# GpSimd multiplies the softmax rows of both attentions of block 2 by their reciprocals, and VectorE evicts every second turned tile of the odd one

## The reference, cut to what matters

```
p = softmax(s)          # exp(s - max) / sum, along the keys
out = p @ v
```

## Time and profile before

| | |
|---|---|
| runs | 1958.44, 1960.0, 1961.77 us, median 1960.0 |
| profiled execution | span 1956.7 us from first to last instruction; the page gives no time of it beside this span |
| TensorE busy | 1913.7 us, 98% of the span |
| VectorE, ScalarE, GpSimd busy | 1273.9, 922.8, 14.1 us |
| chain that ended last | TensorE 92%, VectorE 4%, ScalarE 2% |
| granted TensorE clock | 0.995 on average |
| DMA | 320.62 MB, mean 164 GB/s |

### The profile page before, as it was taken

One profiled execution on the slowest core, in us unless ns is written; L12 is line 12 of the kernel. 1 busy time (PEld: TensorE's weight loads), 2 busy tenths in 40 slices (PEclk: granted clock), 3 DMA queues, 4 the chain that ended last, 5 costly groups with the idle time before them and its releaser, 6 DMA issues.

```text
span 1956.7 us, 28779 instructions
## 1 busy us (share of the span) xinstructions
PE 1913.7 (98%) x11994; PEld 1629.3 (83%) x11994; DVE 1273.9 (65%) x1670; ACT 922.8 (47%) x1300; POOL 14.1 (1%) x17
## 2 busy tenths in 40 slices
PE   7999999999999999999999999999999999989998
PEld 6888969888888888788879878988888889679997
DVE  5776796766676668776664464765554367757774
ACT  5334565334533455643454355543333345755553
POOL 0000000000000000000000110000000000000000
PEclk9999999999999999999999999999999999999999
DMA  7876536765476642776453211222323223024552
GB/s 279 283 274 218 186 105 224 280 257 216 157 277 253 229 174 95 272 274 252 152 174 107 108 44 65 101 94 86 108 86 108 87 86 109 23 86 165 180 194 87
DMA packets 46065, 320.62 MB, mean 164 GB/s; under 512 B 5233, under 2 KB 5361, under 8 KB 7921
## 3 DMA queue, kind: packets, MB, share of 16 engines
q1 hardware_dynamic: 39024, 270.09, 38.4%
q10 hardware_dynamic: 6912, 48.69, 6.5%
HBM read 317.72 MB, written 1.05 MB: 163 GB/s over the span
## 4 chain that ended last, share of the span: by engine, by line
PE 92%; DVE 4%; ACT 2%; issue 1%; DMA 0%; DVEq 0%; ACTq 0%
PE ps L532 89%; PE ps L873 1%; DVE s_big L2181 1%; DVE s_wl L1890 1%; PE ps L734 0%; ACT s_wh L1228 0%; PE ps L711 0%; DVE s_st L2120 0%; ACT s_big L1398 0%; DVE s_tmp L2410 0%; DVE ps L2114 0%; DVE s_X L2386 0%; PE ps L835 0%; DVE s_X L2076 0%; DMA s_X<-in_x 0%
## 5 line engine op out<-in xcount | busy, mean ns | idle before, releaser
L532 PE MATMUL ps<-s_xx,s_wh 128*128 128x512 f32 (+1 forms) x3328 | 899.6, 348 | 11.2 <-DVE s_wl L1960 10.0
L1890 DVE TENSOR_TENSOR s_wl<-s_raw,s_wh 128x2048 fp32r<-128x2048 f32 x213 | 487.4, 2290 | 293.5 <-ACT s_wh L1228 293.4
L532 PE MATMUL ps<-s_xx,s_wl 128*128 128x256 f32 (+1 forms) x2208 | 670.2, 304 | 0.4 <-DVE s_xx L2413 0.4
L532 PEld LDWEIGHTS ps<-s_xx,s_wh 128*128 128x128 f32 x3328 | 579.7, 190 | 106.4 <-DVE s_wl L1960 10.3
L1228 ACT ACTIVATE s_wh<-s_raw 128x2048 fp32r<-128x2048 f32 x213 | 404.7, 1907 | 133.0 <-PE ps L532 129.7
L532 PEld LDWEIGHTS ps<-s_xx,s_wl 128*128 128x128 f32 x2208 | 419.4, 190 | 19.6 <-issue 3.2
L532 PE MATMUL ps<-s_wh,s_hl 128*128 128x512 f32 (+1 forms) x608 | 232.3, 382 | 0.5 <-DVE s_hl L1982 0.5
L532 PE MATMUL ps<-s_wh,s_hh 128*128 128x512 f32 (+1 forms) x608 | 230.0, 378 | 0.0
L532 PE MATMUL ps<-s_wl,s_hh 128*128 128x512 f32 (+1 forms) x608 | 229.8, 378 | 0.0
L532 PE MATMUL ps<-s_wh,s_xx 128*128 128x256 f32 x928 | 179.4, 287 | 0.0
L1342 ACT ACTIVATE s_tmp<-s_tmp 128x512 f32<-128x512 f32 x44 | 27.8, 632 | 281.2 <-DVE s_tmp L2007 274.5
(11 more groups left out here) (235 smaller groups left out, 1680.9 us busy)
## 6 DMA issues: line engine op xcount, KB each, us to landing
s_big<-in_w_ada ACTq DMA_DIRECT2D x46, 1024.0 KB, 6.1
s_raw<-in_ffn_down SPq DMA_DIRECT2D x44, 1024.0 KB, 4.8
s_raw<-in_w_up SPq DMA_DIRECT2D x44, 1024.0 KB, 4.8
s_raw<-in_ffn_gate SPq DMA_DIRECT2D x43, 1024.0 KB, 5.1
s_raw<-in_ffn_up SPq DMA_DIRECT2D x43, 1024.0 KB, 4.8
s_raw<-in_w_down SPq DMA_DIRECT2D x22, 1024.0 KB, 4.8
s_raw<-in_w_in SPq DMA_DIRECT2D x18, 1024.0 KB, 4.8
s_raw<-in_w_in_ab SPq DMA_DIRECT2D x10, 1024.0 KB, 4.8
```

The costliest lines, as they stand in the source:

```text
L532: return pe.matmul(o, lhsT, rhs, start=start, stop=stop, skip_group_check=True)
L1890: dve.tensor_tensor(wide(wl, u), raw[:, u % SLOTS, :].rearrange("p (k n) -> p k n", k=8), f32(wide(wh, u)), SUB).then_inc(*w_low.tick(u))
```

## The change

GpSimd gets a function `weigh(A, u)` that does the multiplications that `unit_divide` did on VectorE, in place and with the same operands, for both attentions; VectorE keeps the reciprocal. A new signal `weighed` is waited for by TensorE before it turns a tile, and by VectorE before it overwrites statistics of eight units earlier. GpSimd's program is ordered by hand: bias additions of heads 0 to 3, `weigh(0)`, heads 4 and 5, `weigh(1)`, `weigh(2)`, heads 6 and 7, `weigh(3)`, and then the rest in order.

In the odd attention (`A.both == 1`) ScalarE evicts only the turned tile of i = 0; VectorE evicts that of i = 1 with a copy, after `unit_maxima(n)` and before `out_low(n-3)`, and raises the new signal `brought`, for which TensorE waits before the values. In the even attention ScalarE keeps both evictions.

```diff
@@ class Attention
-                self.units = []
+                self.units, self.both = [], 2 if name == "even" else 1
@@ tensor, unit_turns
-                    pe.wait_ge(*divided[A.name, u, i])
+                    pe.wait_ge(*weighed[A.name, u, i])
...
-                    freed[b] = turned[A.name, u, i]
+                    freed[b] = (turned if i < A.both else brought)[A.name, u, i]
@@ tensor, unit_values
-                pe.wait_ge(*turned[A.name, u, 1])
+                pe.wait_ge(*turned[A.name, u, A.both - 1])
+                if A.both == 1:
+                    pe.wait_ge(*brought[A.name, u, 1])
@@ scalar, unit_turned
-                for i, hd in A.pair_of(u):
+                for i in range(A.both):
@@ vector, unit_maxima
                     if u >= 8:
-                        dve.wait_ge(*divided[A.name, u - 8, 1])
+                        dve.wait_ge(*weighed[A.name, u - 8, 1])
@@ vector, unit_divide
                 dve.reciprocal(A.stat(u, "over", n=2 * n), A.stat(u, "sum", n=2 * n)).then_inc(
-                    *divided.tick((A.name, u, "r")))
-                dve.wait_ge(*divided[A.name, u, "r"])
-                for i, hd in A.pair_of(u):
-                    for j, (q, off, w) in enumerate(A.parts(u)):
-                        e = A.e(u, i)[:, off:off + w]
-                        dve.tensor_scalar(e, e, A.stat(u, "over", i, j), None, MUL).then_inc(
-                            *divided.tick((A.name, u, i)))
+                    *divided.tick((A.name, u)))
@@ vector, attend
                     unit_maxima(A, n)
+                if A.both == 1 and 2 <= n < len(A.units) + 2:
+                    dve.wait_ge(*product[A.name, "t", n - 2, 1])
+                    if n >= 4:
+                        dve.wait_ge(*product[A.name, "pv", n - 4])
+                    src, dst = A.turn(n - 2, 1)
+                    dve.tensor_copy(dst, src).then_inc(*brought.tick((A.name, n - 2, 1)))
@@ gpsimd
+            def weigh(A, u):
+                pool.wait_ge(*divided[A.name, u])
+                for i, hd in A.pair_of(u):
+                    for j, (q, off, w) in enumerate(A.parts(u)):
+                        e = A.e(u, i)[:, off:off + w]
+                        pool.tensor_scalar(e, e, A.stat(u, "over", i, j), None, MUL).then_inc(
+                            *weighed.tick((A.name, u, i)))
...
+            for h in range(4):
+                bias(h)
+            H = even_heads()
+            for u in range(len(H.units)):
+                if u in (1, 3):
+                    bias(u + 3)
+                    bias(u + 4)
+                weigh(H, u)
+            H = odd_heads()
+            for u in range(len(H.units)):
+                weigh(H, u)
```

More of the change, by code:

```diff
@@ L158, in program @@
         gain_diag, y_out, shifted_low = (signal(n) for n in ("gain_diag", "y_out", "shifted_low"))
-        biased, cleared = (signal(n) for n in ("biased", "cleared"))
+        biased, cleared, weighed, brought = (signal(n) for n in ("biased", "cleared", "weighed", "brought"))
         def const(name):
@@ L411, in pair_of, with turn @@
                 return [(i, self.heads[2 * p + i]) for i in range(2)]
+            def turn(self, u, i):
+                src = ps[self.tbank[i]][:, :]
+                if self.units[u][1] is None:
+                    return (src.rearrange("p (q c t) -> p q c t", q=2, t=128),
+                            self.pt(u, i).rearrange("p c (q t) -> p q c t", t=128))
+                return src.rearrange("p (c t) -> p c t", t=128), self.pt(u, i)
             def ends(self, u):
@@ L1406, in unit_turned @@
                         act.wait_ge(*product[A.name, "pv", u - 2])
-                    src = ps[A.tbank[i]][:, :]
-                    if A.units[u][1] is None:
-                        src, dst = (src.rearrange("p (q c t) -> p q c t", q=2, t=128),
-                                    A.pt(u, i).rearrange("p c (q t) -> p q c t", t=128))
-                    else:
-                        src, dst = src.rearrange("p (c t) -> p c t", t=128), A.pt(u, i)
+                    src, dst = A.turn(u, i)
                     act.activation(dst, src, ACT.Copy).then_inc(*turned.tick((A.name, u, i)))
@@ L2731, in gpsimd, with bias @@
                 pool.memset(U[:, :, 0:16], 0.0).then_inc(*cleared.tick(("u", l)))
-            pool.wait_ge(*cleared["u", 1])
-            pool.wait_ge(*cb_in["two"])
-            for h in range(8):
+            def bias(h):
                 pool.wait_ge(*bias_in[h % 4][h])
@@ L2740, in gpsimd @@
                 pool.tensor_tensor(t, t, both(two("near")), ADD).then_inc(*biased.tick(h))
+            def weigh(A, u):
[5 more added lines that the diff above has]
+                            *weighed.tick((A.name, u, i)))
+            pool.wait_ge(*cleared["u", 1])
+            pool.wait_ge(*cb_in["two"])
+            for h in range(4):
[9 more added lines that the diff above has]
+                weigh(H, u)
         for f in (sync, tensor, scalar, vector, gpsimd):
```

## The result

The changed kernel took 2003.07 us (median of 4 runs, 2001.45 to 2008.27), the kernel before 1959.22 us on the same chip (4 runs, 1958.18 to 1961.77): ratio 1.0226, 95% interval 1.0214 to 1.0239. The sign was forecast, the size was not: 2003 lies far above the range (1958.5 to 1975.6) and above the dearest rival (1979.8).

A forecast was written before the change was run, and what follows sets the result against it. TensorE, busy for 1913.7 of 1956.7 us, was taken as the bound. The span plus 0.5 (even attention) and 6.2 (odd) gave 1963.4, and 3.3 more gave 1966.7 us; range 1958.5 to 1975.6.

The forecast's parts named there:

- the dearest rival: Both attentions: a GpSimd multiplication costs about what its addition does, 1.27 us; +17.3 odd, +2.5 even, 1979.8 us; chance 0.13.
- the price c: Both attentions: time of one GpSimd multiplication of 512 columns, not shown by any row, taken as 0.90 us.
- The upper end of 1.27: GpSimd multiplication: highest price considered, from its addition, which reads two streams and writes one, 1.27 us for 512 columns.
- a dear per-row scalar: GpSimd multiplication: the condition named under which its price would lie above 1.27 us.
- its even half: Even attention: GpSimd's queue lengthens unit 3's stall, last values come later; +0.5 us at c = 0.90, +2.5 at 1.27.
- The odd ring: Odd attention: turning, VectorE's copy, reciprocal, two GpSimd multiplications, next turning; 1.53 + 2c or 1.87 + 2c a unit, +6.2 us.
- splitting the evictions saves nothing: Odd attention's tail: second turned tile is out 1.88 us after the turning's start with VectorE's copy, against 1.83 now.
- ScalarE as the bound after 1173: Even attention: VectorE bounds it up to about 1173, ScalarE after it, as ScalarE works there without a pause.
- the third: Both attentions: GpSimd multiplication at its addition's price, c about 1.27; +17.3 and +2.5 us, 1979.8 us; chance 0.13.
- Those below c = 0.82: Odd attention: no loss at the fill's price (1959.0 us, chance 0.23), or only steps with L2105 late (1961.4, 0.19).
- the fourth: Even attention: all 5.1 us of TensorE's idle time go, with c low; 1954.9 us; chance 0.04.
- the 3.3 us added to the span: Whole kernel: the runs' median of 1960.0 lies 3.3 us above the profiled span, so the same was added to the forecast.

The follow-up runs named there:

- best: Against the kernel before, even attention only: GpSimd multiplies one tile in six units and does four subtractions, VectorE evicts last four units' second tiles; 1959.81 us, +1.5.

## Why the prediction was wrong

**The step that failed is the price c** of one GpSimd multiplication, "The multiplication reads one and writes one; with its streams counted (1, 2, 3) it lies half way, and I take c = 0.90 us". It measures 1.56 us. The streams don't set it: a copy reads and writes as much and takes 0.61, and the product of two tiles takes 1.29. The upper end of 1.27 was an argument by the same count and no bound; the prediction named what would break it, a dear per-row scalar, and gave it no weight (it is the scalar form that is dear, with a constant nearly as much: 1.49). With c = 1.56 and nothing else changed, its own formulas give 72.1 - 46.15 = +25.9 for the odd half (measured +26.8 alone, +27.6 in the change), and its even half, drawn on from +2.5 at 1.27 by 5.4 us per us, +4.1. That is +30.0 of +43.9 us. The missing 13.9 are 8.6 in the even half, 1.7 in the odd intervals, 1.6 from the last turning to its values and 1.4 behind (both partly at a lower clock), and half a microsecond between the two profiled executions (their spans differ by 42.9, and the even half began 0.4 earlier) and the medians.

**The odd ring was right**, in its links, its order and its formula (57.3 and 73.0 against 56.8 and 72.1; no loss at 0.44). So was the claim that splitting the evictions saves nothing: moved alone, it changed nothing. That cutting the ring leaves +4.0 of +28.0 is the proof that it is one.

**The even half was undersized for more reasons**, which its price alone does not mend. The prediction followed each wait once and did not let a late turning come back: two units on, its delay is in the next reciprocal (4.58 + 2c against 6.21). At 0.90 that ring would lose 0.2 us a round, so the forecast of +0.5 was near what it asked for; at 1.56 it loses 1.5 a round. Of the +6.7 up to unit 7 the two units of that ring and the two behind them have 1.1 and 1.6; 2.1 had come up to unit 1, which the prediction did not look at, and 1.9 in GpSimd's queue with the bias additions, which it did. In the last four units four multiplications behind a late reciprocal cost 2.7 us, and the clock 3.2: +5.9.

**The clock.** The earlier trace rows have it at full speed; the prediction kept it there. It fell behind waits of TensorE, though not behind all: 0.66 after 1.03 and 0.92 us at unit 1, but 1.00 after 1.10 and 0.93 at unit 7. The fall at unit 1 cost nothing, as GpSimd had the chain there; 3.2 us of the even half are the later one. No experiment separates it: it comes from two rounds of one trace against the same two before.

**ScalarE as the bound after 1173** was right for a part of the first late wait at most: with its evictions halved 1.27 of 1.48 us stayed, and all of the other two (best). Its row without idle time was read as a load; it was busy, but what TensorE mostly waited for was the way through it.

**Of the rivals** the third was the nearest in kind (a dear price) and had 0.13. Those below c = 0.82, 0.46 of the chance with the fourth, rested on a fill of one stream as evidence for arithmetic.

**A small one:** the 3.3 us added to the span were not the time around it. In the kernel after the profiled run took 2001.45 us with a span of 1999.6, 1.8 around it; the other 1.5 are the spread of the runs.

What stays open: the stretch of 8.49 us before unit 7 has ScalarE and L2345 in its chain, and how much each adds was not tried. The account of the last four units comes from timelines; no run moved their reciprocal. Why GpSimd's scalar form is so dear no run here shows.

## What to carry to other kernels

Price an operation on an engine by a row of that same operation and form; where there is none, a count of streams is not a bound, and the form (scalar, repeated column, copy) can change it by 2.5 times. Before moving work to a slower engine in an in-order pipeline, write each ring through the queues, also the one that returns two units later, as fixed part + n x price against the bound engine's period: GpSimd was idle for 95% of the span and still cost 44 us, and one reciprocal's place in a queue was 24 of 28 us. A wait that stays when its engine has less to do is a latency. Other work put between can fill it, if nothing else is queued behind the place from which it was taken; here it filled 1.1 us in one trace and no gain was measurable in the runs.

## What the runs showed of the hardware

- GpSimd, 128x512 float32, undisturbed: copy 0.61 us, product with a repeated column 1.04, product of two tiles 1.29, multiplication by a constant 1.49, by a per-row column 1.56 (128x256: 0.92 and up). VectorE does the last in 0.44 to 0.49.
- GpSimd and VectorE disturb each other: GpSimd's 1.56 became 1.85 beside a VectorE multiplication of 0.49 that was not slowed; four short VectorE multiplications took 3.18 us instead of 1.14 beside GpSimd's subtractions.
- Two GpSimd multiplications in a row take 3.11 us, twice one: no overlap. A second one is handed to TensorE 0.14 us after its end.
- TensorE's granted clock was 0.53 in 1190 to 1200 of the kernel after, behind 12 us in which it was busy for 8.02, and its instructions took 1.97 instead of 1.09 us. Waits of about a microsecond were followed by a lower clock at unit 1 (0.66) and by the full one at unit 7.
